# Early experts' rows of a sparse MoE: picked into rows and turned, or picked already turned

## The reference

```
h = rmsnorm(x, norm_ffn[i])                     # (512, 1024)
# top-1 of 4 groups, then top-2 of the 8 experts in it; 32 experts, D_EXPERT = 256
combine = sum(one_hot(expert_id, 32) * gate)    # (512, 32), two non-zeros a token
hid = silu(h @ w_gate[e]) * (h @ w_up[e])       # per expert e
x = x + sum_e combine[:, e] * (hid @ w_down[e])
```

## Time and profile before

| what | value |
|---|---|
| median of 3 runs | 1280.29 us (1276.42 to 1282.89) |
| profiled execution | 1278.82 us, its span 1277.1 us, mean granted clock 0.971 |
| PE busy | 1145.1 us, 90% of the span |
| PEld, DVE, ACT, POOL busy | 805.1, 519.5, 383.5, 385.5 us |
| DMA | 278.24 MB, mean 218 GB/s |
| expert part, layer 0 and layer 1 | from about 250 to 490 us, and from about 1011 to 1255 us |

### The profile page before, as it was taken

The page is one execution under the profiler, slowest core; times in us unless marked ns, Lnnn a source line. Parts: engine busy times, 40 slices in busy tenths (PEclk is TensorE's granted clock), DMA queues, the critical chain, the costliest instruction groups (busy, mean ns, idle before and its releaser), DMA issues.

```text
span 1277.1 us, 21577 instructions
## 1 busy us (share of the span) xinstructions
PE 1145.1 (90%) x8755; PEld 805.1 (63%) x8755; DVE 519.5 (41%) x1188; ACT 383.5 (30%) x854; POOL 385.5 (30%) x428
## 2 busy tenths in 40 slices
PE   5999999899999884989889999889999899999782
PEld 4876678655555442868568887678888555555441
DVE  4466663411111114564684455753653411111114
ACT  3426841111111102354553445543422111111010
POOL 1233621112232211047545266542301022322110
PEclk9999999999999997989999999999999899999896
DMA  7121047999999998111000120002366999999996
GB/s 241 67 73 67 2 192 277 368 364 381 383 386 379 383 392 320 69 66 67 2 3 1 67 101 31 3 2 81 151 247 261 359 372 389 388 386 377 380 390 247
DMA packets 67795, 278.24 MB, mean 218 GB/s; under 512 B 16888, under 2 KB 16984, under 8 KB 43120
## 3 DMA queue, kind: packets, MB, share of 16 engines
q1 hardware_dynamic: 56480, 255.89, 52.7%
q0 software_dynamic: 11072, 20.43, 4.7%
q10 hardware_dynamic: 144, 0.52, 0.1%
HBM read 265.83 MB, written 27.26 MB: 230 GB/s over the span
## 4 chain that ended last, share of the span: by engine, by line
PE 69%; DMA 13%; DVE 8%; ACT 4%; SPq 3%; issue 2%; POOL 1%; DVEq 0%; POOLq 0%
PE bank L1132 14%; PE bank L150 9%; PE bank L152 8%; PE bank L151 8%; DMA hn<-in_moe_w_up 8%; PE bank L1141 6%; PE bank L1676 4%; PE bank L1124 3%; DMA x<-in_moe_w_up 3%; SPq L2382 2%; PE bank L541 2%; PE bank L550 1%; PE bank L575 1%; PE bank L389 1%; PE bank L298 1%
## 5 line engine op out<-in xcount | busy, mean ns | idle before, releaser
L1002 POOL DMA_INDIRECT y_rows<-arena,idx_i x64 | 64.5, 1008 | 350.0 <-DVE arena L1319 345.0
L1224 ACT ACTIVATE arena<-bank 128x128 f32<-128x128 f32 x64 | 17.7, 277 | 368.2 <-PE bank L1132 368.2
L1323 DVE TENSOR_TENSOR arena<-arena,bank 128x128 f32<-128x128 f32 x64 | 18.4, 287 | 259.2 <-ACT arena L1224 259.2
L152 PE MATMUL bank<-ring_r,ht_r 128*128 128x512 f32 x288 | 113.0, 392 | 0.0
L1132 PE MATMUL bank<-ring,arena 128*64 128x256 f32 x832 | 101.6, 396 | 7.7 <-DMA ring<-in_moe_w_up 6.7
L1319 DVE COPY arena<-bank 128x512 f32<-128x512 f32 x64 | 44.2, 691 | 144.2 <-PE bank L1141 144.2
L150 PE MATMUL bank<-ring_r,arena_r 128*128 128x512 f32 (+1 forms) x228 | 91.3, 401 | 6.1 <-DVE ring_r L174 5.4
L151 PE MATMUL bank<-ring_r,arena_r 128*128 128x512 f32 x224 | 87.8, 392 | 0.0
L1132 PEld LDWEIGHTS bank<-ring,arena 128*64 128x64 f32 x832 | 57.9, 136 | 42.7 <-DMA ring<-in_moe_w_up 7.7
L151 PE MATMUL bank<-ht_r,ring_r 128*128 128x512 f32 (+1 forms) x224 | 80.9, 361 | 0.0
L1124 PEld LDWEIGHTS bank<-ident,arena 64*128 64x128 f32 x512 | 61.3, 201 | 28.3 <-issue 25.1
(11 more groups left out here) (343 smaller groups left out, 2338.4 us busy)
## 6 DMA issues: line engine op xcount, KB each, us to landing
ring<-in_moe_w_gate SPq DMA_DIRECT2D x26, 1024.0 KB, 21.5
ring<-in_moe_w_up SPq DMA_DIRECT2D x26, 1024.0 KB, 25.3
arena<-in_moe_w_down SPq DMA_DIRECT2D x24, 1024.0 KB, 27.5
ring<-in_moe_w_down SPq DMA_DIRECT2D x24, 1024.0 KB, 26.9
ring<-in_gdn_w_in SPq DMA_DIRECT2D x8, 2048.0 KB, 8.0
arena<-in_moe_w_gate SPq DMA_DIRECT2D x10, 1024.0 KB, 19.4
arena<-in_moe_w_up SPq DMA_DIRECT2D x10, 1024.0 KB, 23.3
ht<-in_moe_w_gate SPq DMA_DIRECT2D x10, 1024.0 KB, 27.0
```

Of the source, the lines that this page charges most:

```text
L152: return pe.matmul(dst, a[1], b[0], start=False, stop=stop)
L1002: pool.indirect_dma_start(out=y_rows[l], out_offset=bass.IndirectOffsetOnAxis(ap=idx_i[:, 1, e:e + 1], axis=0), in_=y_out[:, e % RING, :], ...
```

## The change

For experts 0 and 1 the roles of the two operands are exchanged. `hn[:, t, c::KC]` (128 tokens by every eighth channel, 128 columns) becomes the stationary operand and `picks[0][:, t, :]` (128 slots) the moving one, for each of 8 chunks c and 4 token tiles t: 32 products of 128 columns in place of 8 of 512. What comes out is already channel by slot, which is the layout of `xgt`, so `xg`, the turns and the `take` of these two experts fall away: ACT copies the lower four chunks of each expert and DVE the upper four from PSUM to `xgt`.

```diff
@@ PER
-        PER.update({n: EXPERTS for n in ("st", "turned", "xgt", ...
+        PER.update(turned=EXPERTS - EARLY)
+        PER.update({n: EXPERTS for n in ("st", "xgt", ...
@@ moe_pool
             def gather(e):
-                if e >= AHEAD:
-                    pool.wait_ge(s["turned"], e - AHEAD + 1 + l * PER["turned"])
+                if e >= AHEAD + EARLY:
+                    pool.wait_ge(s["turned"], e - AHEAD - EARLY + 1 + l * PER["turned"])
@@
+        def picked(e, half):
+            return (xgt[:, e, half * 4 * SLOTS:(half + 1) * 4 * SLOTS].rearrange("p (c n) -> p c n", c=4),
+                    pick_bank(half).rearrange("p (c n) -> p c n", c=4)[:, :, e * SLOTS:(e + 1) * SLOTS])
@@ moe_pe
                 pe.wait_ge(pick["made"], PICK["made"] + 1 + l)
-                for t in range(TT):
-                    for half in range(2):
-                        last = pe.matmul(pick_bank(half)[:, :], picks[0][:, t, :], hn[:, t, half * HALF:(half + 1) * HALF],
+                for c in range(KC):
+                    for t in range(TT):
+                        last = pe.matmul(pick_bank(c // 4)[:, c % 4 * P:(c % 4 + 1) * P], hn[:, t, c::KC], picks[0][:, t, :],
                                          start=t == 0, stop=t == TT - 1)
                 last.then_inc(pick["rows"], 1)
 
             def turn(e):
-                if e < EARLY:
-                    pe.wait_ge(pick["kept"], PICK["kept"] + 2 * (l + 1))
-                else:
-                    pe.wait_ge(xg_full[e % AHEAD], rows_in(l, e))
-                if e:
+                pe.wait_ge(xg_full[e % AHEAD], rows_in(l, e))
+                if e > EARLY:
                     pe.wait_ge(s["xgt"], e + l * PER["xgt"])
                 turn_rows(e).then_inc(s["turned"], 1)
@@ body(e)
                 pe.wait_ge(s["xgt"], e + 1 + l * PER["xgt"])
+                if e < EARLY:
+                    pe.wait_ge(pick["kept"], PICK["kept"] + EARLY * l + e + 1)
                 gate_and_up(e % RING, slot).then_inc(s["up"], 1)
-                if e < EXPERTS - 1:
+                if EARLY <= e + 1 < EXPERTS:
                     turn(e + 1)
@@
             pick_rows()
-            turn(0)
             for e in range(EXPERTS):
@@ moe_act
             act.wait_ge(s["idx"], 1 + l * PER["idx"])
-            act.wait_ge(s["pool_c"], 1 + l * PER["pool_c"])
             act.wait_ge(pick["rows"], PICK["rows"] + 1 + l)
-            act.copy(xg[:, 0, 0:HALF], pick_bank(0)[:, :]).then_inc(pick["kept"], 1)
+            for e in range(EARLY):
+                act.copy(*picked(e, 0)).then_inc(s["xgt"], 1)
 
             def take(e):
-                act.wait_ge(s["turned"], e + 1 + l * PER["turned"])
+                act.wait_ge(s["turned"], e + 1 - EARLY + l * PER["turned"])
                 act.copy(xgt[:, e % RING, :], bank[0][:, :]).then_inc(s["xgt"], 1)
 
-            take(0)
             for e in range(EXPERTS):
...
-                if e < EXPERTS - 1:
+                if EARLY <= e + 1 < EXPERTS:
                     take(e + 1)
@@ moe_dve
             dve.wait_ge(pick["rows"], PICK["rows"] + 1 + l)
-            dve.tensor_copy(xg[:, 0, HALF:D], pick_bank(1)[:, :]).then_inc(pick["kept"], 1)
+            for e in range(EARLY):
+                dve.tensor_copy(*picked(e, 1)).then_inc(pick["kept"], 1)
```

More of the change, by code:

```diff
@@ L930, in build @@
                    ranks=1, pos=1, placed=2 * TT, lists=1, idx=1, combined=TT)
-        PER.update({n: EXPERTS for n in ("st", "turned", "xgt", "up", "silu", "hidden", "hid_turned", "hid_t",
+        PER.update(turned=EXPERTS - EARLY)
+        PER.update({n: EXPERTS for n in ("st", "xgt", "up", "silu", "hidden", "hid_turned", "hid_t",
                                          "y_sum", "y_copied")})
```

## The result

| kernel | median us | ratio to before | 95% interval |
|---|---|---|---|
| before | 1281.18 (4 runs) | | |
| the change | 1294.37 (4 runs, 1289.65 to 1296.70) | 1.0106 | 1.0083 to 1.0129 |

The change makes the kernel 13.2 us slower (the interval of the ratio is 10.6 to 16.5 us). I had forecast 1274.7, 5.6 us faster than the runs then known.

A forecast was written before the change was run, and what follows sets the result against it. Bytes at 386 GB/s and DMA time lost in early gaps were taken to bound the expert parts. Gains of 3.0 us in layer 0 and 2.6 in layer 1, together 5.6, took 1280.3 to 1274.7 us; range 1269.5 to 1280.8.

The forecast's parts named there:

- What bounds the kernel: Expert parts, both layers: their end is set by bytes at 386 GB/s plus DMA time lost in three early gaps.
- The picks: Start of each expert part: 64 records at about 0.12 us, 7.65 us in all, ending 0.6 us later than before.
- the slower rival: Picks: loads don't overlap with products; at 0.23 us a record 8.6 us slower, 1288.9 us; chance 0.06.
- From the picks to expert 0: Between last pick and expert 0's gate and up: 0.52 us for copies and hand-overs, in place of 2.6 us.
- The clock: Expert 0's gate and up: PE's clock stays up, so they take 3.85 us in place of 5.44.
- Gaps and sum: Early DMA gaps: gaps 2 and 3 close, gap 1 grows slightly; gains 3.0 and 2.6 us, together 5.6.
- The clock does not pay: Expert 0's gate and up: clock falls again or its earlier fall was accidental; gain 3.6 us, 1276.7 us; chance 0.20.
- PE's lead is the measure: Expert parts: transfers wait for homes PE frees, so PE's whole lead arrives; gain 7.2 us, 1273.1 us; chance 0.10.
- nothing arrives: Last loads of each layer: gaps close but the loads take the time back; 1280.3 us; chance 0.10.

The follow-up runs named there:

- e8: e5 with expert 5's load into hn also held back until expert 0's up product; 1282.66 us, ratio 1.0029 to before.
- e3: The kernel before with only the normed rows of the expert parts written chunk by chunk, so their readers see contiguous columns; 1280.86 us, ratio 0.9993.
- price list: The kernel before with eleven series of 16 extra PE instructions ahead of layer 0's picks, one execution; products 0.115 us a record at step 1, 0.238 at 8.
- e1: The change with contiguous columns in the picks, so experts 0 and 1's channels don't match their weights; 1276.01 us, ratio 0.9955 to before.
- e5: The change with contiguous columns in the picks and experts 0 and 1's gate and up weights laid to match; 1277.23 us, ratio 0.9974 to before.
- e2: The change with the normed rows of the expert parts written chunk by chunk, so all readers see contiguous columns; 1277.87 us, ratio 0.9976 to before.
- e6: e5 with each of the 32 contiguous pick products issued twice; 1292.61 us, ratio 1.0106 to before.
- e7: e5 with nine idle products on PE behind the release of hn; 1279.92 us, ratio 1.0007 to before.

## Why the prediction was wrong

**What bounds the kernel: right.** The rate behind the gaps is unchanged (386 GB/s in layer 0, and 383 from 1034 to 1250 us against 385 from 1028.5 to 1240 before), and e8 shows that a later load costs time with PE undisturbed.

**The picks: wrong, and this is the step that failed.** I priced a record at 0.12 us by the nearest rows: a two-pass product with contiguous columns at 0.115, and a one-pass turn with the 32-byte step at 0.12. Neither row has both, and I took it that what is free in each is free together. It costs 0.239, twice the row. I had this as the slower rival, at 0.06, and its reason was loads that don't overlap with products; the runs give another, the step: products with the step in the moving operand alone cost the same (0.233), and in the change PE and PEld are busy side by side (15.26 and 15.07 of the 15.30 us). At 0.23 a record that rival gave 8.6 us slower. I also wrote that the loads set the pace of the contiguous product; e3's one-pass loads come every 0.07 us, so that this is what sets the pace there is not shown. The trace of before held a warning: the loads for one-pass turns last 139 ns at line 1185 where the columns are contiguous, and 193 at line 298 or 201 at line 1124 where they are 32 bytes apart. I read how often they come, not how long they last; and the pace of line 1124 (eight in 1.09 us) already had the step's price in it, as e3's 0.71 shows.

The Trainium skill has the rule that I should have weighed ("SBUF — State Buffer", Door 1: The DMA port swizzle): a memory line is 16 bytes, and reads run at full bandwidth only with at least two hits to a line. The price list agrees with two hits: float32 at step 2 costs 0.119 us, at step 3 0.175, and from step 4 on 0.23 to 0.24. The same passage of the Trainium skill calls a step of up to 4 float32 values free; here step 4 already costs the full double, so the measurement decides. The rule that I did weigh in the prediction, the Trainium skill's 107 ns for a load of 128 columns, is near the two-pass products at step 1 (0.112 to 0.115), too high for e3's one-pass loads (0.07), and off by more than two at step 8.

**From the picks to expert 0: right.** 0.60 us from the last pick to gate and up, where I had 0.52. The copies of four runs of 64 take the time of 256 columns.

**The clock: right.** Gate and up of expert 0 take 3.84 or 3.85 us in both layers of the change and of every experiment built on it; only e3, which is the kernel before in this, has the 5.44 of before.

**Gaps and sum: right in kind and, for short picks, in size.** e1 gains 5.8 us where the sum had 5.6, and e5 and e2 3 to 3.5; in its trace e5's two expert parts are 5.5 us shorter than before. That e1 comes so close is partly luck, since its gain is known to about 2 us. With the measured 15.27 us of picks in place of 7.65 the prediction's own sum gives 5.6 - 2 x 7.62, 9.6 us slower, and the measured 13.2 lies above it by more than its interval allows (10.6 at least). The size of the record is thus most of the miss, not quite all. In the profiled execution (1296.7 us, 2.3 above its median) the expert parts grew by 5.7 us in layer 0 and 6.6 in layer 1, together 12.3, where the windows give 11.7 (layer by layer they agree less well, 4.2 and 7.5). The other 5.4 us of its longer span lie between the expert parts, where its granted clock was lower (0.90 against 0.96 in the 45 to 49 us ahead of layer 1's picks). e1's profiled execution has the same long stretch, with a clock of 0.89 there, so I put this down to the execution and not to the change. It also bears on the gap: in the 30 us ahead of layer 1's picks the DMA engines moved 343 GB/s, against 313 before, which fits the early fall at 1018: the first loads had landed sooner against the picks. What remains open is small: against e5 the change's expert parts cost 17.8 us for 15.9 us more of picks, where e6's cost 14.4 for 14.3, and one execution of each doesn't tell whether the step has a share in those 2 us.

**The rivals.** "The clock does not pay", "PE's lead is the measure" and "nothing arrives" are each ruled out by a run (e1 with its 3.84 us, e8, e7). The slower rival had the right place and threshold: 0.216 us a record was named as the point from which the kernel is 0.5% slower, and at 0.239 it is 1.1% slower. Its price was somewhat low.

## What to carry to other kernels

Price an operand by a row that has all its properties together: kind of instruction, number of passes, and the step between columns. If no row has them, the range must take in what the untested combination could cost; here that was a factor of two on 64 records. And look whether a row hides the price: the turns of rows with the step looked free at 0.12 us each, and without it they take 0.07 (e3). Turning a layout inside a product is only free if the read is contiguous or nearly so; here it was cheaper to change the order in which two experts' weights are laid down (3 us faster than before) than to read `hn` at a step of 32 bytes (13 us slower). And where a transfer waits for the end of an operand's use, as expert 5's load for `hn`, an instruction ahead of the release delays both the load and PE, and one behind it PE alone: in the expert parts of the traces 14.3 us ahead of it cost 14.4, and 7.2 us behind it 5.6.

## What the runs showed of the hardware that I had not expected

- In float32 products of 128 by 128 the step between columns costs nothing at 8 bytes, half again at 12 and double from 16 on, for the stationary operand; at 32 bytes the moving operand pays the same (0.233 against 0.112 us a record).
- A turn (one record) of columns 32 bytes apart comes every 0.109 us when 128 columns are moved, as one of contiguous columns, though its load lasts 194 ns in place of 140. When 64 are moved the step shows: eight turns take 1.09 us with it and 0.71 without (e3).
- A DVE product of x, a scalar and a gain row over 1024 float32 columns takes about 2.2 us with x and the gain read at a 32-byte step, and 1.28 without (e2).
